# Recurrent heads with half projections between level products, and state space heads in pairs

## The reference

```python
proj = xn @ w_in[l]
(hq, hf, hi, hg, sz, sxbc, sdt, gq, gk, gv, gg, glr, lx, lg, mg) = split(proj)
ya = hgrn2_branch(hq, hf, hi, hg, lb_all[l], hgrn_norm_w[l])   # 4 heads of 128
yb = ssd_branch(sz, sxbc, sdt, ...)                            # 8 heads of 64, 2 groups
yc = gla_branch(gq, gk, gv, gg, glr, ...)                      # 4 heads, keys of 64
yd = rglru_branch(lx, lg, ...)
branch_out = einsum('blnw,nwd->blnd', ys, w_branch[l])
gates = sigmoid(mg).reshape(bsz, seqlen, 4, D_MODEL)
merged = sum(gates * branch_out, axis=2)
```

## Time and profile before

| | |
|---|---|
| Median of 3 runs | 4377.37 us (4374.73 to 4393.15) |
| Profiled execution, its own time | 4373.86 us |
| Its span | 4372.1 us |
| PE busy | 3900.0 us (89%) |
| DVE busy | 1796.2 us (41%) |
| ACT busy | 1283.7 us (29%) |
| POOL busy | 896.6 us (21%) |
| Chain that ended last | PE 74%, DVE 14%, ACT 7%, issue 4% |

### The profile page before, as it was taken

How to read it: one execution, slowest core, us unless ns; L and a number is a source line. 1 busy time by engine, 2 the same in 40 slices (tenths; PEclk the granted TensorE clock), 3 DMA queues, 4 the chain that set the end, 5 groups by cost and what they waited for, 6 DMA issues and landing times.

```text
span 4372.1 us, 51616 instructions
## 1 busy us (share of the span) xinstructions
PE 3900.0 (89%) x21728; PEld 3066.9 (70%) x21728; DVE 1796.2 (41%) x2260; ACT 1283.7 (29%) x1511; POOL 896.6 (21%) x528
## 2 busy tenths in 40 slices
PE   6967998888999999999999889799888799988878
PEld 5756777677778777888888666576676566766657
DVE  5344434435260463111102544636543356555461
ACT  3223333223240111000001233435522466433340
POOL 3201222212132243333333311010012001011101
PEclk8978998978899999999999999899998899999999
DMA  3100111101123442111112211010111000100011
GB/s 126 31 25 25 48 44 48 30 15 39 37 64 107 157 130 72 53 47 50 46 49 87 82 53 44 15 39 11 49 49 45 16 14 25 27 22 22 22 44 58
DMA packets 276489, 215.06 MB, mean 49 GB/s; under 512 B 15984, under 2 KB 254736, under 8 KB 276272
## 3 DMA queue, kind: packets, MB, share of 16 engines
q1 hardware_dynamic: 256400, 146.01, 11.8%
q10 hardware_dynamic: 19872, 65.94, 4.2%
HBM read 170.11 MB, written 37.75 MB: 48 GB/s over the span
## 4 chain that ended last, share of the span: by engine, by line
PE 74%; DVE 14%; ACT 7%; issue 4%; ACTq 1%; DMA 0%; SPq 0%; DVEq 0%; POOL 0%; POOLq 0%
PE ps L324 41%; PE ps L341 15%; DVE AR L1861 4%; DVE AR L1869 2%; PE ps L948 2%; DVE SM L2505 2%; PE ps L561 2%; PE ps L306 2%; PE ps L959 1%; PE ps L377 1%; PE ps L395 1%; PE ps L970 1%; PE ps L283 1%; DVE SM L2439 1%; PE ps L939 1%
## 5 line engine op out<-in xcount | busy, mean ns | idle before, releaser
L2609 POOL CAST WH<-WR 128x1024 fp32r<-128x1024 f32 (+2 forms) x254 | 271.2, 1068 | 3296.6 <-DMA WR<-in_w_in 1054.5
L324 PE MATMUL ps<-XH,WH 128*128 128x512 f32 x2656 | 700.5, 408 | 31.6 <-ACT AR L1354 22.1
L324 PE MATMUL ps<-XH,WL 128*128 128x512 f32 x2656 | 662.3, 392 | 0.0
L324 PE MATMUL ps<-XL,WH 128*128 128x512 f32 x2656 | 656.1, 389 | 0.0
L324 PEld LDWEIGHTS ps<-XH,WH 128*128 128x128 f32 x2656 | 509.1, 195 | 153.0 <-ACT AR L1354 23.1
L2611 POOL TENSOR_TENSOR WL<-WR,WH 128x1024 fp32r<-128x1024 f32 (+2 forms) x254 | 586.7, 2310 | 20.3
L324 PEld LDWEIGHTS ps<-XH,WL 128*128 128x128 f32 x2656 | 500.3, 188 | 111.9
L324 PEld LDWEIGHTS ps<-XL,WH 128*128 128x128 f32 x2656 | 494.2, 186 | 108.2
L1861 DVE TENSOR_TENSOR AR<-AR 128x512 f32<-128x512 f32 (+2 forms) x345 | 385.7, 1118 | 65.5 <-ACT AR L1193 32.9
L341 PE MATMUL ps<-ARR,WH 128*128 128x512 f32 x1600 | 394.2, 392 | 16.0 <-ACT ARR L1480 8.4
L341 PEld LDWEIGHTS ps<-ARR,WH 128*128 128x128 f32 x1600 | 301.8, 189 | 82.5 <-issue 9.5
(11 more groups left out here) (237 smaller groups left out, 4516.1 us busy)
## 6 DMA issues: line engine op xcount, KB each, us to landing
WR<-in_w_in SPq DMA_DIRECT2D x78, 512.0 KB, 3.8
WR<-in_w_ffn_in SPq DMA_DIRECT2D x44, 512.0 KB, 3.8
spill<-H ACTq DMA_DIRECT2D x32, 512.0 KB, 2.7
gates<-AR ACTq DMA_DIRECT2D x32, 512.0 KB, 3.1
AR<-gates SPq DMA_DIRECT2D x32, 512.0 KB, 3.4
H<-spill ACTq DMA_DIRECT2D x32, 512.0 KB, 7.7
WR<-in_w_in_e SPq DMA_DIRECT2D x26, 512.0 KB, 3.9
WR<-in_w_in_o SPq DMA_DIRECT2D x23, 512.0 KB, 3.9
```

Source lines behind the costliest of these rows:

```text
L324: mm = pe.matmul(pt[0:m, h * 512:h * 512 + 512], wp[:, slot, k, 0:m], xp[:, k, h * 512:h * 512 + 512], start=i == 0, stop=i == 3 * KD - 1)
L2609: pool.tensor_copy(hi, full).then_inc(s_whi, 1)
```

## The change

State space heads: mask and decay get a second buffer each (A(12), A(14) beside A(25), A(26)), DVE's work on a head is cut into `ssd_differ` and `ssd_weigh` and done in pairs; four `seg` come first, then two behind each y; a gate is projected before each of the first three y. Squares go to A(4) to A(7), so the norm of group 1 can wait until after k of unit 0. Projection z 3 moves behind the B transposes. The softplus of lambda moves from behind the heads to the start of the kernel, on ACT and DVE.

Recurrent units: g, v, q and a gate are projected in halves, a half behind each level product or around U; k goes behind the output. Two-head units put both heads' level products in one PSUM tile. There are 21 gates ahead of the last block instead of 16: one more in the state space stage, two more in each two-head unit.

```diff
-        FILL = {1: {0: [("g", 0)], 2: [("v", 0)], 4: [("vt", 0)]},
-                2: {-1: [("g", 0)], 0: [("g", 1)], 1: [("v", 0)], 2: [("vt", 0), ("v", 1)], 4: [("vt", 1)]}}
+        FILL = {1: {4: [("vt", 0)]}, 2: {}}
+        LATE = {1: {3: [("g", 0)], 4: [("v", 0)], 6: [("vt", 0)]},
+                2: {1: [("g", 0)], 3: [("g", 1)], 4: [("v", 0)], 5: [("vt", 0)], 6: [("v", 1)]}}
...
+            def xhalves(name, src):
+                pt, n = opn(name)
+                pe.wait_ge(freed[n % 4], n // 4)
+                w = weight(src, n)
...
+                for h in range(2):
...
+                    if h:
+                        mm.then_inc(filled[n % 4], 1)
+                    yield
...
-            for f in range(4):
+            for f in range(3):
                 xgemm(("z", f), cols(win, SZ + f * P))
...
             transposes(("Bt",), A(12))
+            xgemm(("z", 3), cols(win, SZ + 3 * P))
...
-            seg(0)
-            seg(1)
+            for h in range(4):
+                seg(h)
             for f in range(4):
                 if f < 3:
-                    seg(2 * f + 2)
-                    if f == 2:
-                        spread(("ynb", 0), A(28))
-                    if f % 2 == 0:
-                        mg()
+                    mg()
                 else:
                     gla_q(0)
+                if f == 2:
+                    pe.wait_ge(s_ysq, 2)
+                    sums(("yn", 0), "w256", [A(4), A(5)])
...
-                if f < 3:
-                    seg(2 * f + 3)
...
+                if f < 2:
+                    seg(2 * f + 4)
+                    seg(2 * f + 5)
+                elif f == 2:
+                    spread(("ynb", 0), A(0))
             gla_k(0)
+            pe.wait_ge(s_ysq, 4)
+            sums(("yn", 1), "w256", [A(6), A(7)])
...
+                    if u == 0 and l < 0:
+                        spread(("ynb", 1), A(0))
...
+                    if u >= 4:
+                        if l < 0:
+                            xgemm(("g", u, 0), cols(win, gc[0]))
+                            mg()
+                        elif l == 0:
+                            half = xhalves(("g", u, 1), cols(win, gc[1]))
+                        elif l == 2:
+                            half = xhalves(("v", u, 0), cols(win, vc[0]))
+                        elif l == 4:
+                            pe.wait_ge(freed[bank(("v", u, 0))], turn(("v", u, 0)))
+                            transposes(("vt", u, 0), A(24))
+                            half = xhalves(("v", u, 1), cols(win, vc[1]))
+                        elif l == 6:
+                            pe.wait_ge(freed[bank(("v", u, 1))], turn(("v", u, 1)))
+                            transposes(("vt", u, 1), A(24))
+                            GU[u] = gates_done[0]
+                            half = mg_halves()
+                        if l >= 0:
+                            next(half)
+                    if u < 4 and l >= 0:
+                        if l in (0, 2, 5):
+                            half = xhalves(("g", u, 0), cols(win, gc[0])) if l == 0 else \
+                                xhalves(("v", u, 0), cols(win, vc[0])) if l == 2 else mg_halves()
+                        if l != 4:
+                            next(half)
...
                 if u < 4:
-                    gla_q(u + 1)
+                    half = xhalves(("q", u + 1), cols(win, HQ + (u + 1) * P if u < 3 else GQ))
+                    next(half)
...
-                if u < 4:
-                    gla_k(u + 1)
+                next(half)
...
-                    if u == 4 and hh:
+                    if u < 4:
+                        gla_k(u + 1)
+                    elif hh == 0:
+                        half = mg_halves()
+                        next(half)
+                    elif u == 4:
                         gla_q(u + 1)
...
-                    if hh == nh - 1:
-                        GU[u] = gates_done[0]
-                        mg()
                     pe.wait_ge(freed[bank(("o", u, hh))], turn(("o", u, hh)))
                     sums(("on", u, hh), "w128", [A(21)])
+                    if u >= 4 and hh == 0:
+                        next(half)
```

On ACT (the heads, and the reading out in a unit; `leave` is the old reading of g, v and vt, now by `LATE`):

```diff
+            def ssd_decay(h):
+                if h >= 2:
+                    act.wait_ge(s_mc, h - 1)
...
+            for fz in range(-1, 4):
+                if fz < 3:
+                    ssd_decay(2 * fz + 2)
+                    ssd_decay(2 * fz + 3)
+                    ssd_mask(2 * fz + 2)
+                    ssd_mask(2 * fz + 3)
...
+                if fz == 2:
+                    seeds(("yn", 0), A(0))
+                if fz < 3:
+                    gate_store(28)
...
-                if u == 4:
+                if u < 4:
+                    gate_store(10)
+                elif u == 4:
                     gla_k(u + 1)
                 elif u == 5:
                     lru_x(0)
                     block_diagonal()
+                if u >= 4:
+                    gate_store(10)
```

On DVE the heads, and the level products of two heads in one tile:

```diff
+            for k in range(-1, 4):
+                if k >= 0:
+                    ssd_weigh(2 * k)
+                    ssd_weigh(2 * k + 1)
+                if k < 3:
+                    ssd_differ(2 * k + 2)
+                    ssd_differ(2 * k + 3)
...
+                        if l < 0 or hh == nh - 1:
+                            step.then_inc(freed[bank(name)], 1)
```

More of the change, by code:

```diff
@@ L359, in xgemm, with mg_halves @@
                 three(pt, w % 4, m).then_inc(filled[n % 4], 1)
+            def xhalves(name, src):
+                pt, n = opn(name)
+                pe.wait_ge(freed[n % 4], n // 4)
+                w = weight(src, n)
+                splits.append(("weight", w, P, 8))
+                nsplit[0] += 1
+                pe.wait_ge(s_wsplit, nsplit[0])
+                for h in range(2):
+                    passes = [(k, WH, XH) for k in range(KD)] + [(k, WL, XH) for k in range(KD)] \
+                        + [(k, WH, XL) for k in range(KD)]
+                    for i, (k, wp, xp) in enumerate(passes):
+                        mm = pe.matmul(pt[:, h * 512:h * 512 + 512], wp[:, w % 4, k, :],
+                                       xp[:, k, h * 512:h * 512 + 512], start=i == 0, stop=i == 3 * KD - 1)
+                    if h:
+                        mm.then_inc(filled[n % 4], 1)
+                    yield
+            def mg_halves():
+                g = gates_done[0]
+                gates_done[0] += 1
+                return xhalves(("mg", g), cols(win, MG + g * P))
             def transposes(name, src, p=P, m=P):
@@ L547, in _ @@
                     banks = []
-                    for hh in range(nh):
+                    for hh in range(nh if l < 0 else 1):
                         pt, n = opn(("P", u, l, hh))
@@ L553, in _ @@
                         c = slice(t * P, t * P + P)
-                        for hh, (pt, n) in enumerate(banks):
+                        for hh in range(nh):
                             r = slice(hh * dk, hh * dk + dk)
                             if l < 0:
+                                pt, n = banks[hh]
                                 mm = pe.matmul(pt[:, c], x1[r, c], x2[r, c], start=True, stop=True)
@@ L1235, in _ @@
             act.wait_ge(s_nega, tick(s_nega))
+            act.activation(SM[:, 4:8], PAR[:, PC["lam"]:PC["lam"] + 4], ACT.Abs).then_inc(s_act_step, 1)
+            act.wait_ge(s_act_step, tick(s_act_step))
+            act.activation(SM[:, 4:8], SM[:, 4:8], ACT.Exp, scale=-1.0).then_inc(s_lsp_in, 1)
+            act.wait_ge(s_lsp_in, tick(s_lsp_in))
             def ssd_silu(k):
@@ L1263, in _, with ssd_gate @@
             ssd_silu(5)
-            for k in range(4):
+            def ssd_gate(k):
                 act.wait_ge(filled[bank(("z", k))], turn(("z", k)))
@@ L1268, in _ @@
                 act.wait_ge(freed[bank(("z", k))], turn(("z", k)))
+            for k in range(3):
+                ssd_gate(k)
             act.wait_ge(s_dec_in, 1)
@@ L1369, in gla_k, with leave @@
                 act.wait_ge(freed[bank(("k", u))], turn(("k", u)))
-            act.wait_ge(s_ys, 4)
+            def leave(kind, u, hh):
+                name = (kind, u, hh)
+                act.wait_ge(s_ys, 4 + u if u < 4 else 8 + 2 * (u - 4))
+                act.wait_ge(filled[bank(name)], turn(name))
+                dst = {"g": [A(26), A(14)], "v": [A(24), A(24)], "vt": [A(25), A(13)]}[kind][hh]
+                act.activation(dst, PS[bank(name)][:, :], other(ACT.Silu) if kind == "g" else ACT.Copy)\
+                    .then_inc(freed[bank(name)], 1)
+                act.wait_ge(freed[bank(name)], turn(name))
+            act.wait_ge(s_mc, 8)
             gla_q(0)
+            act.wait_ge(filled[bank(("y", 3))], turn(("y", 3)))
             gla_k(0)
+            gate_landed()
+            seeds(("yn", 1), A(0))
             for u in range(6):
@@ L1400, in _ @@
                         gate_store(10)
```

(12 more changed lines are left out.)

155 lines of the change are left out of this document (72 added, 83 removed).

## The result

The kernel after took 4186.43 us (median of four runs, 4181.56 to 4190.93), the kernel before 4378.16 (four runs beside them, 4374.73 to 4393.15): ratio 0.9556, 95% interval 0.953 to 0.9581, 192 us less. Forecast were 4170, in a range of 4130 to 4235. The profiled execution took 4181.56 us, its span is 4179.8.

The account below looks back on a forecast made before the run. From 200 to 1140 us PE was taken as bound, losing time to idling and half clock. Terms 54.4 + 65 + 54 + 30 = 203.4 off the profiled 4373.86 gave 4170 us, range 4130 to 4235.

Parts of the forecast that it names:

- Tail: Last block of gates: five of sixteen gates go early, 5 x 10.88 = 54.4 us off the block.
- State space heads: First seg to first gate of unit 0: 98.6 instead of 159.8 us; with z 3, 65 us saved, one more gate included.
- One-head units: Units 0 to 3, first gate of unit 0 to first g of unit 4: 436.6 instead of 490.9, 54 us saved.
- Wait (a): Level 0 of one-head units waits for the new unit's scans and exponents: 1.84 idle, 5.3 us with slower work.
- wait (b): Level 5 of one-head units waits for an exponent queued on ACT behind v's copy: 1.3 idle, 2 of clock.
- rival 4: The waits at levels 0 and 5 and before o cost no clock: some 35 us back, 4135; chance 0.1.
- Two-head units: Units 4 and 5, two more gates each: 141.8 and 154.8 us, 30 saved, bounds 15 and 45.
- the new wait before o: Units 4 and 5: o of head 0 needs the gate's bank; 2.4 idle, 8 us with slower work.
- wait for the first product's bank: Unit 5: the gate behind g 0 needs this bank and waits; 4.3 us, and 3 of clock.
- Rival 1: DVE becomes the bound through POOL's weight splits: half of 42 levels lose 2.7, 57 us, 4227; chance 0.14.
- Rival 2: The clock does not come back: 4 us per level over 42 levels, 138 more, 4308; chance 0.05.
- Rival 3: Slower ring of banks: each level waits for a bank's release; with 6 each, 252 us, 4422; chance 0.03.

Follow-up runs that it names:

- best: Kernel after with four edits: gate ahead of U, v copied later, unit 5's gate ahead of its first product, spread inside the gate; 4137.68 us, ratio 0.9452.
- gate_first: Kernel after with the gate's second half ahead of U and the projection behind it in units 4 and 5; 4171.6 us, ratio 0.9512.
- v_later: Kernel after with ACT copying v behind the exponent of level 5 instead of in front, in one-head units; 4181.1 us, ratio 0.954.
- spread_inside: Kernel after with the spread of units 0 to 2 put inside the gate, after 32 of its 48 matmuls; 4175.48 us, ratio 0.954.
- after_again: The kernel after, unchanged, run once more for the spread of its parts; 4182.53 us, ratio 0.9544 to the kernel before.
- pool_twice: Kernel after with one more elementwise POOL instruction for every weight split in units 0 to 5; 4211.57 us, ratio 0.9612.
- gate5_ahead: Kernel after with spread and one gate of unit 5 ahead of its first product instead of behind g 0; 4173.11 us, ratio 0.9516.
- gates_back: Kernel after without the four early gates of the two-head units, 15 instead of 11 in the last block; 4218.88 us, ratio 0.9629.

## Why the prediction was right, and where not

**The method.** I took PE's busy time times the mean clock as its work at full clock, 99.8 us for a one-head unit from the earlier trace rows. The kernel best, whose units 1 and 2 have no wait at all, takes 100.0: for these units the estimate is right to 0.2 us. For the two-head units it is not. Unit 4 in gate_first and unit 5 in best, each from its g 0 to the next unit's or stage's, have no wait either:

```profile
721.88:860.23 138.35, 138.35 (x870) 112.09 (x868) 64.10 (x73) 46.44 (x46) 33.56 (x19) 1.00 0.17 49
```

```profile
857.71:992.58 134.87, 134.87 (x834) 109.58 (x832) 57.01 (x60) 39.60 (x39) 33.24 (x18) 1.00 0.16 48
```

The first has both extra gates, the second only one, as the other stands ahead of g 0 there; with its 10.88 it is 145.8. I had 111 + 21.8 = 132.8 and 118 + 21.8 = 139.8, so these two terms of work were 5.5 and 6.0 too small. A reason that fits, but that no run isolates: the mean clock of a stretch takes in the idle time too, and in the idle stretch from 863.1 to 872.5 of the kernel before it was 0.66 where the whole unit had 0.83, so that the clock under the work was higher than the mean.

**Tail.** 54.40 by the chain, as forecast. Nothing else bounded the block, in any of the kernels (10.88 a gate throughout).

**State space heads.** 64.0 with z 3, forecast 65. Done alone they gave 74.4, that is with one gate of the tail. PE no longer waits for a y; the largest of the waits left there are 1.68 and 2.20 behind k 0, which I had at 3.4 together, and 1.29 and 1.04 before segs, where I had 1. The move of the softplus cost nothing that any row shows.

**One-head units.** Here the mechanism was right and the price of the clock too high. Wait (a) measured 1.84 and 1.85 in units 1 to 3 and 2.80 in unit 0, wait (b) 1.20 in all four (forecast 1.3). The term that failed is the loss behind them: I charged 3.5 behind (a) and 2 behind (b) in every unit, from the one row. What came in unit 1 is this:

```profile
419.90 2.58 PE L587 MATMUL ps<-AR 128*128 128x64 f32 x16 [1.84 <-DVE AR L1938]
422.23 3.16 PE L373 MATMUL ps<-XH,WH 128*128 128x512 f32 x8
...
454.64 2.00 PE L587 MATMUL ps<-AR 128*128 128x64 f32 x16 [1.20 <-DVE AR L1938]
456.45 2.10 PE L373 MATMUL ps<-XH,WH 128*128 128x512 f32 x8
```

0.6 and 1.05 behind the first, nothing behind the second. In unit 0 it was more (3.36 and 3.76 behind the first, 3.46 behind the second), in unit 3 nothing. The eight waits make 13.1 us, where I had 14.6. With 100.0 for the work of a unit that leaves, as an estimate, some 13 of the 426.0 for the clock and the gate rank projection, where I had charged 23 (4 x 5.5 and 1). That makes the 426.0 instead of 436.6; the second profile of after has 429.3. My rival 4 (the waits cost no clock) had half of the truth. v_later and spread_inside show both causes: take away the copy of v, and (b) goes; take the spread earlier, and (a) goes in units 1 to 3.

**Two-head units.** 303.0 against 296.6, 21.5 saved instead of 28 (I put 30 in the sum, between that and what the matmul rows gave). The term that failed here is the work: 11.5 too small over both units, as shown above. The losses were smaller than charged. Unit 4 lost 146.0 - 138.4 = 7.6 (I had 9): the new wait before o came as forecast, 2.53 (2.4), with o at half clock, and gate_first shows it to cost 7.3 (I had 8); the gate behind g 0 was hidden. Unit 5 lost 157.0 - 145.8 = 11.2, where I had 15. Its wait before o was 1.21, not 2.4, and no clock was lost behind it, for which I had charged 8. Its wait for the first product's bank was longer, 7.43 (9.6 to 9.8 in five of the other kernels) instead of 4.3. I had taken that from a row of before and not asked what DVE does ahead of reading that bank. It does this, while POOL splits the weights for the projections:

```profile
872.39 3.30 DVE L1946 SCALAR_TENSOR_TENSOR AR<-AR 128x1024 f32<-128x1024 f32 x1
```

The same instruction took 1.22 at 407.86, and the DVE chain of the unit's start is late by these 2.1. In after_again POOL's splits met other instructions of that chain (2.78 instead of 0.69 at 877.47, 4.00 instead of 2.13 at 887.90), and the wait was 9.55.

**Rival 1** got 0.14. As it was put, a stall at half of the levels, it did not occur: PE waits for DVE at levels 0 and 5 only, for reasons that were counted. pool_twice shows where more work of POOL bites: one instruction more per weight costs 24 to 29 us, at the starts of units and not at inner levels. **Rival 2** fell with the clock, 0.95 (unit 0) and more in all stages. **Rival 3**, waits for a bank at each level, did not occur; the 7.43 above is the one wait of that kind in the units, beside those before o.

**From 203.4 to 192.** The sum until the first branch product is right to 1.6 us, in part by luck: the one-head units saved 10.9 more than their term and the two-head units 8.5 less. That the median is 4186 and not 4170 comes from behind: 12.7 us in code that is untouched, and 4.9 from the profiled execution to the median of after. I summed against the profiled execution of before, which was at the fast end of its runs and short in that part. In the repetition before and after differ by 202.5. I said that the profiled execution lay 3.5 below the median; the lesson is that it may lie low in a part that the change never meets, and that this belongs in the range. The prediction also says that the clock is 1.00 and PE hardly pauses before and behind the stretch that it treats. That holds from 1140 us to the first branch product (0.99), but not before 200 (0.91, PE busy for 157.6) nor from the first branch product on (0.96, 270 us of idling), and it is in the latter that the 12.7 us arose, for which the sum had no term.

## What to carry to other kernels

When the bound is one engine with a clock that follows its load, an independent piece of work put into its gaps costs less than its own length: two gates of 10.88 us in unit 4 cost nothing there, because they removed 12.3 us of idling and some 10 us lost to the half clock; two in unit 5 cost 8 to 9. Cut the filler as fine as the gaps come (here by halves, once after two thirds), and give the reader of a buffer a whole step between the filler and the next use. And take short waits away together: with one gone, the clock sometimes fell at the next; with nearly all gone, units ran at clock 1.00. An estimate of work as busy time times mean clock held where PE idled 13 of 124 us, and was 5 to 6 us short where it idled 21 and 27 of some 160.

## What the runs showed of the hardware

- Equal waits on PE were followed by a fall of the granted clock or not. Behind 1.21 us of idling before o of unit 5, the matmul pairs stayed at 0.48 in after, after_again and pool_twice, and went to 0.79 in gate5_ahead 1.9 us later, for 7.2 us, with a granted clock of 0.50. Behind 1.20 at level 5 the first group of the half projection took 2.10 in most units and 3.4 to 3.7 in others. In gates_back the clock stood at 0.50 for the 10.3 us of o of head 1, with PE busy throughout.
- 15422 equal matmuls took 2657.7 to 2675.4 us of PE's time, and their stretch 2933 to 2949 us, in the executions of twelve kernels that share them.
- Eight scans of 128x128 on DVE took 3.63 us undisturbed (after, unit 5), 6.37 beside one POOL split (after, at 409.12) and 7.88 beside a split with one more instruction (pool_twice, at 524.67).
- A POOL multiply of 128x1024 took 2.08 us (mean of 42 in pool_twice), the subtract 2.53 and the converting copy 1.17.
